# Attention outputs made turned in a two-layer transformer kernel: values stationary, probabilities of all queries moving, head pairs interleaved

## What is computed

```python
s = einsum('bqhd,bkhd->bhqk', q, k) * scale + bias_or_mask
p = softmax(s, axis=-1)
o = einsum('bhqk,bkhd->bqhd', p, v).reshape(B, S, H * Dv)
y = o @ w_out
```

## Time and profile before

| | us |
|---|---|
| median of 3 runs | 1269.72 |
| lowest and highest | 1268.07 to 1270.68 |
| the profiled execution, its own time | 1268.25 |
| its span in the trace | 1266.4 |
| PE busy in the span | 1039.3 |
| DVE, ACT busy | 377.2, 210.4 |

### The profile page before, as it was taken

How to read it: one execution, slowest core, us unless ns; L and a number is a source line. 1 busy time by engine, 2 the same in 40 slices (tenths; PEclk the granted TensorE clock), 3 DMA queues, 4 the chain that set the end, 5 groups by cost and what they waited for, 6 DMA issues and landing times.

```text
span 1266.4 us, 13963 instructions
## 1 busy us (share of the span) xinstructions
PE 1039.3 (82%) x5243; PEld 579.1 (46%) x5243; DVE 377.2 (30%) x873; ACT 210.4 (17%) x449; POOL 85.5 (7%) x144
## 2 busy tenths in 40 slices
PE   5999998876676666699999998899999999544664
PEld 3545533332221111345566544678878878111121
DVE  1694212143010000335613126322222222233113
ACT  2214201221100000202524121111111111000000
POOL 3000010101000000000000000110011010221000
PEclk9999998987888888799999997799999999677887
DMA  9551568896999999932688858789999997999993
GB/s 287 204 199 67 198 219 313 316 402 248 419 421 421 422 422 420 333 121 83 236 303 321 304 215 360 310 313 356 354 360 349 358 364 257 416 417 419 422 422 131
DMA packets 71147, 395.78 MB, mean 313 GB/s; under 512 B 16924, under 2 KB 19240, under 8 KB 39176
## 3 DMA queue, kind: packets, MB, share of 16 engines
q1 hardware_dynamic: 56056, 329.58, 66.5%
q0 software_dynamic: 11888, 54.19, 12.0%
q10 hardware_dynamic: 3168, 11.54, 2.2%
HBM read 347.05 MB, written 49.19 MB: 313 GB/s over the span
## 4 chain that ended last, share of the span: by engine, by line
PE 64%; DMA 25%; DVE 5%; ACT 2%; issue 2%; SPq 1%; ACTq 0%; DVEq 0%; POOLq 0%; POOL 0%
PE bank L775 27%; DMA wring<-in_w_pack 22%; PE bank L987 13%; PE bank L998 6%; PE bank L943 4%; PE bank L786 3%; PE bank L924 3%; PE bank L819 2%; PE bank L1024 2%; PE bank L802 2%; SPq L471 1%; DMA wring<-in_pack_z.0 1%; DMA PR<-xn_dram,token_now 1%; DVE PT L2037 1%; ACT PT L1366 1%
## 5 line engine op out<-in xcount | busy, mean ns | idle before, releaser
L775 PE MATMUL bank<-wring,hT 128*128 128x512 f32 (+3 forms) x608 | 251.3, 574 | 8.3 <-DVEq L1563 3.8
L924 PE MATMUL bank<-wring,kT 128*32 128x512 f32 x800 | 121.5, 766 | 82.0 <-DMA wring<-in_w_pack 77.9
L775 PEld LDWEIGHTS bank<-wring,hT 128*128 128x128 f32 x608 | 114.2, 200 | 136.1 <-issue 127.3
L987 PEld LDWEIGHTS bank<-qT,wring 128*128 128x128 f32 x1408 | 163.4, 195 | 13.3 <-issue 13.3
L987 PE MATMUL bank<-qT,wring 128*128 128x128 f32 x1408 | 163.6, 278 | 2.8 <-DVE qT L2027 2.8
L924 PEld LDWEIGHTS bank<-wring,kT 128*32 128x32 f32 x800 | 28.8, 136 | 172.6 <-DMA wring<-in_w_pack 94.5
L998 PE MATMUL bank<-wring,PT 128*128 128x512 f32 x176 | 81.4, 605 | 1.3
L943 PE MATMUL bank<-wring,kiT 128*32 128x512 f32 x416 | 63.9, 769 | 18.6 <-DMA wring<-in_w_pack 16.7
L775 PE MATMUL bank<-wring,yT 128*128 128x512 f32 x160 | 71.1, 597 | 1.6 <-issue 0.9
L2037 DVE TENSOR_TENSOR PT<-bank,PT 128x256 f32<-128x256 f32 x22 | 9.3, 424 | 192.9 <-ACT PT L1366 192.9
L2027 DVE TENSOR_SCALAR qT<-bank,gs,modc 128x128 f32<-128x128 f32 x184 | 60.8, 402 | 4.4 <-PE bank L975 3.6
(11 more groups left out here) (362 smaller groups left out, 999.9 us busy)
## 6 DMA issues: line engine op xcount, KB each, us to landing
wring<-in_w_pack SPq DMA_DIRECT2D x174, 1024.0 KB, 19.3
wring<-in_w_pack SPq DMA_DIRECT2D x22, 2048.0 KB, 9.4
y_dram<-gateB SPq DMA_DIRECT2D x8, 4096.0 KB, 19.5
wring<-in_w_ada POOLq DMA_DIRECT2D x24, 1024.0 KB, 7.1
y_dram<-PR ACTq DMA_DIRECT2D x22, 512.0 KB, 9.1
wring<-in_pack_z.0 SPq DMA_DIRECT2D x1, 2048.0 KB, 12.7
wring<-in_pack_z.2 SPq DMA_DIRECT2D x1, 2048.0 KB, 20.7
wring<-in_pack_z.3 SPq DMA_DIRECT2D x1, 2048.0 KB, 8.7
```

The source lines that it names most:

```text
L775: mm = nc.tensor.matmul(b[:, 0:n], lhs(k, t), w[:, k, c0:c0 + n], start=(k == 0), stop=(k == nk - 1))
L924: mm = nc.tensor.matmul(bank[lane[j], 0, :], xqT[:, k, lane[j]], w[:, (k % 4) * 512:(k % 4 + 1) * 512], start=(k == 0), stop=(k == KD - 1))
L987: mm = nc.tensor.matmul(bank[:, 2, f * P:(f + 1) * P], item_gate_up(s)[:, k, f * P:(f + 1) * P], xT[:, s, k, :], start=(k == 0), stop=(k = ...
```

## The change

- Scores, and the index scores, of even and odd heads are interleaved: two banks are opened together, one for even and one for odd heads, and the matmuls alternate between them (`halves_of_rows`). In `score_heads` pairs of groups now cover the same range of heads.
- The probabilities are multiplied by the reciprocal of their sums on DVE (`scaled_probs`) ahead of the transposes, in two halves of the heads, each with a signal.
- `PR` and `PT` lie in one tensor `PRT`. The turned probabilities of tile 1 go where the probabilities of tile 0 were (`PT_both`), so both tiles are there together.
- `outputs` runs once for both tiles: the values are stationary (64 columns for each of two heads side by side, in `mem` 128) and the turned probabilities of 256 queries move. In `dsa` the second key tile moves 128 queries alone. The result has the layout of `yT`, and ACT copies it there in two groups, `o.0` and `o.1`.
- `outputs_turned`, its transposes and `yn` in this role go, and so does ACT's wait for the outputs of tile 0.
- In `mem` ACT's `mod_row(1)` now comes behind the copies of the outputs. Ahead of the experts of the first block TensorE waits for `items1` and no more for `tokens1`.

```diff
-            def outputs(name, t, v, heads, dv, nk):
-                pieces = prob_pieces(heads, nk)
-                copied(pe, f"{name}.p.{t}.{len(pieces) // 4 - 1}")
-                b = opened(f"{name}.o.{t}")
-                for n, (h, kt) in enumerate(pieces):
-                    mm = nc.tensor.matmul(b[:, h * dv:(h + 1) * dv], PT[:, n, :], v(h, kt),
-                                          start=(kt == 0), stop=(kt == nk // P - 1))
-                closed(mm)
+            def outputs(name, v, heads, dv, causal=False):
+
+                copied(pe, f"{name}.p.1.{heads // 2 - 1}")
+                lanes = P // dv
+                for half in range(2):
+                    b = opened(f"{name}.o.{half}")
+                    for c in range(2):
+                        for kt in range(2):
+                            for lane_ in range(lanes):
+                                h = (2 * half + c) * lanes + lane_
+                                t0 = 1 if causal and kt == 1 else 0
+                                mm = nc.tensor.matmul(b[lane_ * dv:(lane_ + 1) * dv, c * S + t0 * P:(c + 1) * S], v(h, kt),
+                                                      PT_both[:, t0:2, 2 * h + kt, :], start=(kt == 0), stop=(kt == 1), skip_group_check=causal)
+                    closed(mm)
...
+            def halves_of_rows(name, i, listed, q, k, t, nk):
+
+                even, odd = opened(f"{name}.{i}"), opened(f"{name}.{i + 1}", 1)
+                for j, (h0, h1) in enumerate(zip(listed[i], listed[i + 1])):
+                    first = nc.tensor.matmul(even[:, j * nk:(j + 1) * nk], q(h0, t), k(h0, nk), start=True, stop=True)
+                    second = nc.tensor.matmul(odd[:, j * nk:(j + 1) * nk], q(h1, t), k(h1, nk), start=True, stop=True)
+                closed(first)
+                closed(second)
...
             def probs_turned(name, t, heads, nk):
                 pieces = prob_pieces(heads, nk)
-                pe.wait_ge(E("probs_made"), attend_value(name, t))
-                for i in range(len(pieces) // 4):
+                turns = len(pieces) // 4
+                for i in range(turns):
+                    pe.wait_ge(E("probs_scaled"), scaled_value(name, t, 2 * i // turns))
                     turn(f"{name}.p.{t}.{i}", [PR[:, t, h, kt * P:(kt + 1) * P] for h, kt in pieces[4 * i:4 * i + 4]])
...
-            def outputs(name, t, heads, dv):
-                key = f"{name}.o.{t}"
-                b = flat(arrived(key), heads, dv)
+            def scaled_probs(name, t, heads, nk):
+
+                dve.wait_ge(E("probs_made"), attend_value(name, t))
                 inv = st[:, 416 + 8 * t:416 + 8 * t + heads]
                 link(V.reciprocal(inv, inv))
-                drained(V.tensor_tensor(yn[:, t, :].rearrange("p (h w) -> p h w", h=heads), b,
-                                        over(inv.unsqueeze(2), [P, heads, dv]), ALU.mult), key)
+                for c in range(2):
+                    hs = slice(c * heads // 2, (c + 1) * heads // 2)
+                    o = PR[:, t, hs, 0:nk]
+                    V.tensor_tensor(o, o, over(inv[:, hs].unsqueeze(2), [P, heads // 2, nk]), ALU.mult).then_inc(E("probs_scaled"), 1)
```

More of the change, by code:

```diff
@@ L798, in scores @@
             def scores(name, t, q, k, heads, nk, paired):
-                for i, hs in enumerate(score_heads(heads, nk, paired)):
+                listed = score_heads(heads, nk, paired)
+                if paired:
+                    for i in range(0, len(listed), 2):
+                        halves_of_rows(f"{name}.s.{t}", i, listed, q, k, t, nk)
+                    return
+                for i, hs in enumerate(listed):
                     b = opened(f"{name}.s.{t}.{i}")
@@ L1047, in index_scores, with key_half @@
                 nk = (t + 1) * P
[L1048 to L1053, removed]
+                listed = score_heads(HEADS, nk, True)
+                def key_half(h, n):
+                    return kiT[64 * (h % 2):64 * (h % 2) + 64, 0:n]
+                for i in range(0, len(listed), 2):
+                    even, odd = opened(f"idx.{2 * t + i}"), opened(f"idx.{2 * t + i + 1}", 1)
+                    for j, (h0, h1) in enumerate(zip(listed[i], listed[i + 1])):
+                        first = nc.tensor.matmul(even[:, j * nk:(j + 1) * nk], pair(qiT)(h0, t), key_half(h0, nk), start=True, stop=True)
+                        second = nc.tensor.matmul(odd[:, j * nk:(j + 1) * nk], pair(qiT)(h1, t), key_half(h1, nk), start=True, stop=True)
+                    closed(first)
+                    closed(second)
             def both_columns(name, jobs_, lhs, t, c0):
@@ L1172, in _ @@
             copied(pe, "gate.3")
-            copied(pe, "tokens1")
+            copied(pe, "items1")
             quads(1, None)
@@ L1441, in _ @@
             copy("kv.1.1", vm[:, 1, :])
+            outputs("dsa", yT[:, 4:8, :])
             for t in range(2):
                 turned4(f"kmT.{t}", kmT[:, :, t * P:(t + 1) * P])
-            for t in range(2):
-                outputs_turned("dsa", t, yT[:, 4:8, :])
             norm_x("x2", tmp)
@@ L1457, in _ @@
                 probs_turned("mem", t, XH, S)
+            outputs("mem", yT[:, 0:4, :])
             mod_row(1)
             mod_columns(1)
-            for t in range(2):
-                outputs_turned("mem", t, yT[:, 0:4, :])
             gate_copied(0)
@@ L1527, in _ @@
             y_columns(7, 1, ACT.Sigmoid)
-            for t in range(2):
-                outputs_turned("mla", t, yT[:, 4:8, :])
+            outputs("mla", yT[:, 4:8, :])
             for t in range(2):
@@ L2154, in _ @@
             ready("km")
-            for t in range(2):
-                outputs("dsa", t, HEADS, HD)
             add_and_turn("wout", "x2", col("xattn_norm"))
```

88 lines of the change are left out of this document (40 added, 48 removed).

## The result

The changed kernel takes 1251.11 us (median of 4 runs, 1248.02 to 1253.54), the kernel before 1268.89 us (4 runs, 1266.33 to 1270.68): ratio 0.986, 95% interval 0.9829 to 0.9891. The forecast was 1252.5 us. In later rounds the same kernel took 1248.70 us (5 runs) with before at 1267.40, so the difference repeats to 1 us and the level to 2.5. The profiled execution took 1249.56 us, 18.7 less than the 1268.25 of before; the sum of the prediction was 17.25.

A forecast was written before the change was run, and what follows sets the result against it. TensorE was taken to bound the attentions, transfers the first block's experts. Savings of 1.6 + 1.25 + 4.1 + 0 + 5.5 + 4.8 = 17.25 us gave 1252.5 us; the forecast's own range was 1249.5 to 1256, with rivals 1248.5 to 1260.

The forecast's parts named there:

- Index scores: Index scores with even and odd heads paired: 4.61 us become 3.0, saving 1.6 us.
- `dsa`, scores and outputs: In `dsa`, scores fall from 4.07 to 2.8 us (saved 1.25); outputs, transposes and a wait save 4.1 us.
- `na`: In `na`, scores fall from 4.91 to 3.65 us, outputs with transposes from 7.9 to 3.65; together 5.5 us saved.
- `mla`: In `mla`, 9.4 us from outputs to `pmla` become 3.65 us and one ACT copy of 0.95; 4.8 us saved.
- `mem`: In `mem`, cheaper outputs against a 1.4 us wait for ACT's `modT.1`: net +0.2 us, called 0; bounds −1.2 and +0.7.
- Scaling on DVE: Scaling a tile of probabilities costs DVE 2.7 us, formerly 0.9; nobody waits, with 3 us left in `na`, the tightest place.
- Loads in the open: Rival, chance 0.07: each paired step in `dsa`, `na`, `mla` waits 0.11 us for its stationary load; 5.3 us more, 1257.8.
- Columns serial: Rival, chance 0.05: 64-wide column tiles run one after another; `na` and `mla` lose 3.45 us each, `dsa` 2.6; 1262.0.
- First block swallowed: Rival, chance 0.09: transfers swallow the 6.95 us saved ahead of 205 us in the first block; 1259.4 us.
- Slower: Rival, chance 0.03: the array doesn't overlap when sides change every two passes, so paired scores and outputs become serial; 1281 us.

The follow-up runs named there:

- 16 + 16 kernel: The changed kernel with the outputs of all even heads first (16 passes, both banks), then of all odd heads: 1258.51 us (4 runs).
- the last experiment: The changed kernel with three waits taken apart and two modulation steps moved into TensorE's idle time ahead of the `mem` queries' turn: 1244.70 us (5 runs), ratio 0.9816.
- passes made three times over: The changed kernel with the passes of the `dsa` outputs made three times, same values into the same bank: median 1251.09 us.

## Why the prediction was right, step by step

The mechanisms stood, and the terms of the sum came out within about 0.3 us.

- Index scores: 1.6 forecast, 1.52 measured. `dsa`, scores and outputs: 5.35 and 5.47. `na`: 5.5 and 5.31, with scores at 3.65 and outputs at 3.60. `mla`: 4.8 and 5.11; the wait for ACT's copy is 0.70 us and not 0.95, and the outputs 3.63.
- `mem`: 0 forecast, with a wait of 1.4. The wait is 1.18 us. From the last weight wait to `wo` it is 16.30 us against 15.69 in before (229.77 to 245.46); 0.65 of that are the eight passes at the start, at a lower clock (1.94 us against 1.29). So the edit itself cost nothing. That the whole stretch from the `mem` scores to `wo` kept its length, 28.17 and 28.13 us, is in part luck: the waits for weights were shorter (3.4 us against 4.8) and the clock lower.
- Scaling on DVE: priced at 2.7 us, in after a tile of `na` is 0.20 + 2.36 us, and nobody waits. The root came 3.3 us later by the old base (4 to 5 forecast), so the slack behind it was not 3 us but 4.8. Timelines of DVE and of ACT in after:

```profile
604.59 0.20 DVE L1692 RECIPROCAL st<-st 128x8 f32<-128x8 f32 x1
604.82 2.36 DVE L1696 TENSOR_TENSOR PRT<-PRT,st 128x1024 f32<-128x1024 f32 x2
```

```profile
612.65 0.23 ACT L1316 ACTIVATE st<-st 128x32 f32<-128x32 f32 x1 [4.49 <-DVEq L1576]
...
614.68 2.06 ACT L1307 ACTIVATE PRT<-bank 128x512 f32<-128x512 f32 x4
```

- Loads in the open: no. The outputs of `na` and `mla` would have taken over 4.5 us and took 3.60 and 3.63, which leaves 0.15 us beyond 16 steps of 0.216. The Trainium skill ("TensorE: Matmul & The Clock Gate", "The mechanism" in Part 3) has one line by which a weight load overlaps running matmuls only where its row group is another, on which the prediction drew; a sentence ahead of it also lets a load for the background weight buffer be pulled ahead. Here two column tiles of 64 share all rows and their loads are hidden. The measurement decides against the "only"; which buffer the loads used, no trace shows.
- Columns serial: no (3.6 against 6.9), and the 16 + 16 kernel puts 7 us of time behind it.
- First block swallowed: no, for all that lies ahead of `wout`. The reason that I gave fits the traces: POOL's issues wait for TensorE's steps (`<-PE bank L1047`), and the load whose wait ended last ahead of the `mem` outputs was issued at 222.32 us in before and at 214.38 in after. The limit of it is the last experiment: within the stretch of those steps the transfers set the time.
- Slower: the alternation at a grain of two passes is the best of the three grains tried, not the worst. My doubt was the wrong way round: many passes of a side in a row cost the overlap, as the other side begins only four passes ahead.

The 1.4 us by which the profiled execution was better than the sum are the start (0.65) and small pieces of transfers and clock. In the experts' stretch the kernel after began its gather 5.6 us earlier, not the 7 of the forecast, as about 2.4 us had gone to a lower clock between `route1` and the tokens, and made 1.7 us good behind the last expert (14.0 us from its last matmuls to the next block's transposes, against 15.7). I can't call either an effect of the change.

## What to carry to other kernels

Small matmuls that use half of the array's rows or columns are to be written in turn, one half and the other, matmul by matmul: the same passes took 3.6 us with 2 of a side in a row, 4.6 with 8 in a row and 6.3 with 16. It is worth turning a product round so that the narrow operand becomes the stationary one, if that also removes transposes, and a normalisation moved to an idle engine is free up to a slack that can be bounded from the trace before. Before moving work out of TensorE's way, see whether the transfers behind it are released by TensorE: then a gain ahead of them goes through. One among them was lost in the one trace that tried it.

## What the runs showed of the hardware

**A wait on TensorE can cost more than itself.** 2.9 us of waiting for ACT cost 4.6 us, as the clock was at the 1.2 GHz level for most of the 3.6 us behind it. This is one execution. The waits of 1.1 us ahead of the `na` scores and 0.7 behind the `mla` outputs left it at 1.00 in after.

**The clock falls in different places in equal code.** Chains of waits at the routing scores of the second token tile: of after, and of the kernel with 3.7 us more on DVE, the same code up to there. Both have the same waits of 1.3 us ahead.

```profile
260.72 1.97 PE bank L1187 x16
...
263.20 1.35 DVE hT L1640 x2
...
264.59 3.65 PE bank L1187 x16
```

```profile
261.76 1.97 PE bank L1187 x16
...
264.24 1.30 DVE hT L1640 x2
...
265.59 1.99 PE bank L1187 x16
```

From `route1` to the ranks it is 11.0 us in five of the study's fourteen traces and 12.3 to 13.9 in the others; from the last expert's last matmuls to the next block's transposes 14.0 or 15.7 us. Such steps of about 1.7 us are probably much of the scatter of single runs (5 us within most kernels), and a reason why the 5 us of passes made three times over could not be told by four runs while the trace showed them.

**Passes don't start in program order.** The Trainium skill ("TensorE: Matmul & The Clock Gate", "The mechanism" in Part 3) says that matmuls start and end strictly in program order. In the 16 + 16 kernel all passes of the even heads stand ahead of all of the odd ones, and yet pairs start together around the change of side, which two passes of one half never do: the first four odd passes start beside the last four even ones. The measurement decides.
